# Compacting the first group's token rows with float32 products instead of split parts, with unread TensorE passes around the ranking

## The chip, the cores and the metric

One core of a Trainium2 chip (trn2) runs the whole program. The metric is the device time of one execution in microseconds (us), lower is better. The engines named below are TensorE (PE, with its weight loads PEld), VectorE (DVE), ScalarE (ACT), GpSimd (POOL) and SyncE (SP), which here only issues DMAs.

## What is computed

One step of a one-layer streaming encoder for 384 tokens of width 1024 (256 of a prompt, 128 of a decode batch): a combined projection, three attention-like branches, gates, an output projection with residual, and then a hierarchical mixture of experts. The change lies between the last two:

```python
x = x + merged @ w_out
return x + hier_moe(rmsnorm(x, g_norm2), ...)

def hier_moe(h, ...):
    lg = (t @ w_rg + b_rg).astype(F32)
    oh_g = one_hot(argmax(lg), N_GROUPS)          # top 1 of 4 groups
    le = (t @ w_re + b_re) ; le_sel = le of the chosen group
    top_v, top_i = lax.top_k(le_sel, TOP_K)       # top 2 of its 8 experts
    comb = p(group) * softmax(top_v) on these experts
    out = sum over experts of (silu(t @ w_g) * (t @ w_u) * comb) @ w_d
```

An expert has gate and up weights of 1024 x 256 each and down weights of 256 x 1024, all float32.

## The kernel before, in words

All engines walk through two lists written out in Python, `schedule()` for everything up to the routing and `moe_schedule()` for the experts. Each engine runs the same list and takes from it only its own operations, in that order, so an entry's place sets the order in every queue. Semaphores tie the engines together.

**Products.** The dense projections split each operand into a high part in the reduced type fp32r and a low part (the rest) and make three single-pass products of them (L1579 to L1581). Expert products, logits and transposes use plain float32 (L1919, L1942, L1847).

**The end of `schedule()`.** The output projection runs in two halves of 512 columns; its last weight granule is followed by the second residual (DVE L1287), the transposes of x2 (PE L1839), the norm (DVE L1294 to L1296) and the second half of the logits (PE L1847). `x_parts` splits the residual rows x2 into x_hi and x_lo: half 0 by ACT (L1068) and DVE (L1301); of half 1 the high part by ACT, while PE subtracts it (`second_low`, L1598 with the identity as float32, L1599 with the negated identity as fp32r) and ACT copies the result out (L1072). `route` is `route_group` on DVE (L689 to L707: which of the 4 groups each token takes; L693 writes that one-hot for PE) and, on PE, `token_ranks` (L1590, L1592: how many earlier tokens took the same group). DVE reads these ranks at L704.

**The start of `moe_schedule()`.** The up to 128 tokens of a group are its "opening set" of rows. DVE builds a 0/1 matrix pick_g that maps tokens to the group's slots (L1313). PE multiplies it with the rows of x2, for group 0 out of x_hi and x_lo (`compact`, L1880, three token tiles by two parts for each 512 columns); ACT scales the result by the token's norm into xg_hi (L1082), DVE makes xg_lo (`compact_low`, L1324). Meanwhile DVE finds the two best experts (`best`, L678 to L721), PE ranks the tokens in each expert (L1590 again), DVE turns the ranks into slots (`slots`, L727 to L734), PE brings slots and weights into the group's order (`info`, L1890), DVE builds pick_rows (L1353, L1354), and PE gathers and turns the rows for the first four experts (`gather`, L1905), which ACT (L1103) and DVE (L1361) bring out of PSUM into xs.

**The experts.** 16 pairs: gate and up products in two halves (L1919, `gu` and `gu_rest`), silu and weight, transposes (L1928), down products (L1942), scatter back (L1951). The weights come as 96 pieces of 1 MB through a ring of 17 slots; SP issues them in order (L786). Pieces 0 to 11 go out during the output projection. Piece 15 waits for both compactions (L873), since it lands where x2 lies. From piece 17 on each waits until the piece 17 places before has been used: by the first gate/up half (`gu_half`), the second (`gu_ready`) or the down products (`dn_ready`) of its pair.

```python
old = c - PIECES
sp.wait_ge((gu_half, gu_ready, dn_ready)[old % 6 // 2], old // 6 + 1)
```

Of the kernel before, what the change touches and what calls it, by code (L numbers as in the profile page):

```python
# [26 lines left out]
ALU = mybir.AluOpType  # L27
# [5 lines left out]
P = 128  # L33
# [49 lines left out]
def schedule():  # L83
# [143 lines left out]
    s += [("x_parts", 0), ("logits", 0)]  # L227
    granule(b + 3)
    s += [("residual", 1), ("squares2", 1), ("turn_x2", 1), ("norm2",), ("logits", 1), ("x_parts", 1), ("route",)]
# [3 lines left out]
def moe_schedule():  # L233
# [16 lines left out]
    step("compact", 0, 1, 1)  # L250
    s.append(("compact_low", 0, 0, 0, None))
    plain("slots", 0)
    s.append(("compact_low", 0, 1, 1, None))
# [64 lines left out]
def program(nc, io):  # L318
# [4 lines left out]
    with ctx:  # L323
# [39 lines left out]
        def sm(n):  # L363
# [82 lines left out]
        x_hi = [[at(f"x_hi{n}{t}", [P, 512], (o_raw, o_ot)[n] + 2 * KB * t, F32R) for t in range(T)] for n in range(2)]  # L446
        x_lo = [[at(f"x_lo{n}{t}", [P, 512], ((o_raw + 6 * KB, o_raw + 8 * KB, o_raw + 10 * KB), (o_ot + 6 * KB, o_ot + 8 * KB, o_h + 8 * KB))[n][t], F32R)
                 for t in range(T)] for n in range(2)]
        xs = at("xs", [P, 2, KT, 256], o_raw)
        neg_ident = at("neg_ident", [P, P], o_z + 111 * KB, F32R)  # L450
# [54 lines left out]
        out_tile, xlo_psum = sem("out_tile"), sem("xlo_psum")  # L505
        gate_ready, br_mul, br_add, mt_ready, mt_hi, mt_evac, x2_ready, ss2_ready, rstd2_ready = (sem(n) for n in ("gate_ready", "br_mul", "br_add", "mt_ready", "mt_hi", "mt_evac", "x2_ready", "ss2_ready", "rstd2_ready"))
        x2t_ready, x2t_even, x2t_odd, lg_ready, route_in, route_exp, taken_ready, rank_ready, info_in = (sem(n) for n in ("x2t_ready", "x2t_even", "x2t_odd", "lg_ready", "route_in", "route_exp", "taken_ready", "rank_ready", "info_in"))
        rows_ready, rows_out, xhi_ready, xparts_ready, pick_ready, gather_done, xs_even, xs_odd, gu_ready = (sem(n) for n in ("rows_ready", "rows_out", "xhi_ready", "xparts_ready", "pick_ready", "gather_done", "xs_even", "xs_odd", "gu_ready"))
# [386 lines left out]
        def _(act):  # L895
            for kind, *arg in steps:
# [165 lines left out]
                elif kind == "x_parts":  # L1062
                    if i == 0:
                        act.activation(neg_ident[:, :], ident, ACT.Copy, scale=-1.0)
                        act.wait_ge(lo_ready, NGRAN)
                    act.wait_ge(x2_ready, T * i + T)
                    for t in range(T):
                        act.activation(x_hi[i][t][:, :], x2[:, t, 512 * i:512 * i + 512], ACT.Copy).then_inc(xhi_ready, 1)  # L1068
                    if i == 1:
                        for t in range(T):  # L1070
                            act.wait_ge(xlo_psum, t + 1)
                            act.activation(x_lo[i][t][:, :], ps[:, t, :], ACT.Copy).then_inc(xparts_ready, 1)  # L1072
# [501 lines left out]
        def _(pe):  # L1574
# [26 lines left out]
            for kind, *arg in steps:  # L1601
# [251 lines left out]
                elif kind == "route":  # L1853
                    token_ranks(0, 32, 4, [T * NR + 4 * t for t in range(T)])
                    second_low(2)
# [258 lines left out]
```

## Time and profile before

| | us |
|---|---|
| median of 3 runs | 685.89 |
| lowest and highest run | 685.65, 686.43 |
| the profiled execution, its own time | 685.87 |
| its span in the profile | 684.1 |
| DVE, ACT, POOL busy | 348.6, 255.9, 117.8 |
| bytes moved, mean rate | 176.65 MB, 258 GB/s |

The rows further down come from this one profiled execution. In a timeline a row is the start, the duration, the engine, the line of the code, the operation, what it writes and reads, its shape and how often, and in brackets how long the engine had been idle before and on whom it had waited. Start times count from the start of the span. A float32 product shows as two records on PE, an fp32r product as one. A matmul's record is longer than its share of the engine, because consecutive ones overlap; the spacing of the starts is the price of one in a stream.

### The profile page before, as it was taken

How to read it: one execution, taken by the hardware profiler on the slowest of the kernel's cores; microseconds unless marked ns; L12 is line 12 of the kernel's file. 1: busy time of each engine (PE TensorE's matmuls, PEld its weight loads, DVE VectorE, ACT ScalarE, POOL GpSimd, SP SyncE). 2: the span in 40 equal slices, each digit the busy share in tenths (PEclk: the TensorE clock that was granted, in tenths of full speed). 3: DMA queues.
4: the chain of work that ended last, by engine and by line, in shares of the span. 5: the costliest groups of instructions: out<-in, count | busy, mean ns of one | idle time of the engine just before them, and what ended most of it. 6: DMA issues, size and time to landing. Idle time of an engine off the chain costs nothing.

```text
span 684.1 us, 9466 instructions
## 1 busy us (share of the span) xinstructions
PE 647.9 (95%) x3518; PEld 430.2 (63%) x3518; DVE 348.6 (51%) x743; ACT 255.9 (37%) x495; POOL 117.8 (17%) x128
## 2 busy tenths in 40 slices
PE   5999999998999999999999999978999999999985
PEld 4887888877788776777777878753433443343321
DVE  4649348985446555554445755565434344343212
ACT  5673343336324545455854334321211221221100
POOL 0019426652001110000000010002101201201100
PEclk9999999999999999999999999999999999999999
DMA  8966342354123632213676479978999999999991
GB/s 313 409 239 211 129 131 94 142 202 140 63 85 130 224 125 98 89 62 124 248 276 262 138 248 423 405 306 333 425 420 419 421 422 419 421 423 419 422 418 54
DMA packets 34703, 176.65 MB, mean 258 GB/s; under 512 B 4272, under 2 KB 4416, under 8 KB 21472
## 3 DMA queue, kind: packets, MB, share of 16 engines
q1 hardware_dynamic: 31696, 164.86, 61.8%
q0 software_dynamic: 2960, 11.16, 4.7%
q8 instruction: 30, 0.49, 0.3%
q14 instruction: 17, 0.14, 0.1%
HBM read 167.47 MB, written 9.06 MB: 258 GB/s over the span
## 4 chain that ended last, share of the span: by engine, by line
PE 78%; issue 8%; DVE 6%; DMA 4%; ACT 2%; POOL 0%; POOLq 0%; SPq 0%; DVEq 0%; ACTq 0%
PE banks L1919 14%; PE banks L1579 14%; PE banks L1581 13%; PE banks L1580 13%; PE banks L1942 8%; DMA piece<-in_wexp 4%; PE banks L1905 2%; PE banks L1773 1%; PE banks L1746 1%; PE banks L1787 1%; PE banks L1847 1%; DVE xs L1361 1%; DVE act_T L1389 1%; PE banks L1747 1%; PE banks L1765 1%
## 5 line engine op out<-in xcount | busy, mean ns | idle before, releaser
L1160 DVE TENSOR_TENSOR w_lo<-raw,w_hi 128x1024 fp32r<-128x1024 f32 (+1 forms) x81 | 128.5, 1597 | 87.9 <-ACT w_hi L926 87.7
L1579 PE MATMUL banks<-w_hi,hT_hi 128*128 128x512 f32 x312 | 124.0, 397 | 1.5 <-ACT z L953 0.9
L1581 PE MATMUL banks<-w_hi,hT_lo 128*128 128x512 f32 x312 | 121.6, 390 | 0.0
L1580 PE MATMUL banks<-w_lo,hT_hi 128*128 128x512 f32 x312 | 121.6, 390 | 0.0
L1919 PE MATMUL banks<-piece,xs 128*64 128x512 f32 x512 | 116.1, 594 | 3.0 <-DMA piece<-in_wexp 2.9
L926 ACT ACTIVATE w_hi<-raw 128x1024 fp32r<-128x1024 f32 x79 | 83.4, 1056 | 88.6 <-PE banks L1581 84.5
L1919 PEld LDWEIGHTS banks<-piece,xs 128*64 128x64 f32 x512 | 37.8, 137 | 77.5 <-issue 69.7
L1579 PEld LDWEIGHTS banks<-w_hi,hT_hi 128*128 128x128 f32 x312 | 58.6, 188 | 15.3 <-issue 2.0
L1581 PEld LDWEIGHTS banks<-w_hi,hT_lo 128*128 128x128 f32 x312 | 58.6, 188 | 12.4
L1580 PEld LDWEIGHTS banks<-w_lo,hT_hi 128*128 128x128 f32 x312 | 58.6, 188 | 11.4
L1942 PE MATMUL banks<-piece,act_T 128*64 128x512 f32 x256 | 60.2, 613 | 1.2 <-DVE act_T L1389 0.3
L1394 DVE SCALAR_TENSOR_TENSOR act_h<-banks,rt,act_g 128x256 f32<-128x256 f32 x16 | 7.7, 484 | 76.2 <-ACT act_g L1109 76.1
L1377 DVE TENSOR_TENSOR y_lo<-banks,y_hi 128x512 fp32r<-128x512 f32 x32 | 20.6, 686 | 48.7 <-ACT y_hi L1114 48.7
L1114 ACT ACTIVATE y_hi<-banks 128x512 fp32r<-128x512 f32 x32 | 17.4, 595 | 74.4 <-PE banks L1942 74.4
L1942 PEld LDWEIGHTS banks<-piece,act_T 128*64 128x64 f32 x256 | 17.3, 139 | 34.9 <-issue 29.2
L1109 ACT ACTIVATE act_g<-banks 128x256 f32<-128x256 f32 x16 | 6.2, 385 | 84.8 <-PE banks L1919 84.8
L1551 POOL TENSOR_SCALAR back<-slotrow,const 128x128 fp32r<-128x128 f32 x16 | 10.0, 627 | 121.3 <-ACT slotrow L1088 60.3
L1579 PE MATMUL banks<-w_hi,oT_hi 128*128 128x512 f32 x72 | 28.9, 401 | 1.4 <-DVE oT_lo L1272 1.4
L1581 PE MATMUL banks<-w_hi,oT_lo 128*128 128x512 f32 x72 | 28.1, 390 | 0.0
L1580 PE MATMUL banks<-w_lo,oT_hi 128*128 128x512 f32 x72 | 28.1, 390 | 0.0
L953 ACT ACTIVATE z<-banks,small 128x512 f32<-128x512 f32 x39 | 23.8, 683 | 4.6 <-PE banks L1581 3.0
L997 ACT ACTIVATE p_sb<-s_sb,small 128x256 f32<-128x256 f32 (+1 forms) x24 | 11.4, 475 | 32.0 <-DVE small L1250 32.0
(340 smaller groups left out, 979.8 us busy)
## 6 DMA issues: line engine op xcount, KB each, us to landing
piece<-in_wexp SPq DMA_DIRECT2D x96, 1024.0 KB, 19.5
raw<-in_wstream SPq DMA_DIRECT2D x79, 512.0 KB, 4.2
foxc<-in_foxc POOLq DMA_DIRECT2D x8, 512.0 KB, 4.9
memv<-in_memc SPq DMA_DIRECT2D x8, 512.0 KB, 4.8
memk<-in_memc SPq DMA_DIRECT2D x8, 512.0 KB, 4.9
xT<-in_xT SPq DMA_DIRECT2D x1, 1536.0 KB, 11.5
xtok<-in_xtok SPq DMA_DIRECT2D x1, 1536.0 KB, 7.8
x<-in_xtok SPq DMA_DIRECT2D x1, 1536.0 KB, 6.2
```

Of the source, the lines that this page charges most:

```text
L926: act.activation(w_hi[:, i % PART_SLOTS, :], raw[:, i % RAW_SLOTS, :], ACT.Copy).then_inc(hi_ready, 1)
L953: act.activation(dst[:, t, :], ps[:, bank_of(i, t), :], f, scale=sc).then_inc(acc_evac if last else tile_evac[t], 1)
L997: act.activation(p_sb[:, i % 2, 0:n], src, ACT.Exp, bias=nmax[:, i % 2:i % 2 + 1], accum_out=rsum[:, i % 2:i % 2 + 1]).then_inc(u_exp, 1)
L1114: act.activation(y_hi[:, 512 * n:512 * n + 512], ps[:, 5 + n, :], ACT.Copy).then_inc(yhi_ready, 1)
L1160: dve.tensor_tensor(w_lo[:, i % PART_SLOTS, cols], raw[:, i % RAW_SLOTS, cols], w_hi[:, i % PART_SLOTS, cols].bitcast(F32), ALU.subtract). ...
L1377: dve.tensor_tensor(y_lo[:, cols], ps[:, 5 + n, :], y_hi[:, cols].bitcast(F32), ALU.subtract).then_inc(ylo_ready, 1)
L1579: mm(out, xh, wh, start=start, stop=False, skip_group_check=True)
L1580: mm(out, xh, wl, start=False, stop=False, skip_group_check=True)
L1581: return mm(out, xl, wh, start=False, stop=stop, skip_group_check=True)
L1905: ins = mm(ps[:, b0, 256 * k2:256 * k2 + 256], x[:, k * P:(k + 1) * P], pick[:, :], start=x is xg_hi, stop=x is xg_lo, **kw)
L1919: ins = mm(ps[64 * e2:64 * e2 + 64, 2 + a % 2, :], xs[:, (a // 2) % 2, k, c0:c0 + CAP], piece[c % PIECES][:, 512 * (k % 4):512 * (k % 4) + ...
L1942: ins = mm(ps[64 * e2:64 * e2 + 64, 5 + n, :], act_T[:, a % 2, f * P + 64 * e2:f * P + 64 * e2 + 64], piece[c % PIECES][:, o:o + 512], sta ...
```

## The change

`x_parts` is dropped: no x_hi, x_lo or negated identity is made, on any engine. `compact` multiplies pick_g, read as float32, with x2 itself, three float32 products for each 512 columns in place of six fp32r ones; it no longer waits for parts. The compaction of the second 512 columns is moved behind `slots` in the list of the experts, so behind the ranks of the experts on PE and behind the slots on DVE. PE gets products whose result nobody reads (384 columns, fp32r, into bank 3): six behind the second half of the logits and four behind the ranks of the groups, where `second_low` was. In the overflow branch the count that PE waits for is lowered to match; that branch isn't taken in these runs. The diff:

```diff
--- before.py
+++ after.py
@@ -224,9 +224,9 @@
     granule(b + 1)
     s.append(("turn_x2", 0))
     granule(b + 2)
-    s += [("x_parts", 0), ("logits", 0)]
+    s.append(("logits", 0))
     granule(b + 3)
-    s += [("residual", 1), ("squares2", 1), ("turn_x2", 1), ("norm2",), ("logits", 1), ("x_parts", 1), ("route",)]
+    s += [("residual", 1), ("squares2", 1), ("turn_x2", 1), ("norm2",), ("logits", 1), ("route",)]
     return s, units
 
 
@@ -247,9 +247,9 @@
     plain("info", 0)
     plain("best", 0, 1)
     step("compact", 0, 0, 0)
-    step("compact", 0, 1, 1)
     s.append(("compact_low", 0, 0, 0, None))
     plain("slots", 0)
+    step("compact", 0, 1, 1)
     s.append(("compact_low", 0, 1, 1, None))
     plain("info", 1)
     plain("pick", 0)
@@ -443,11 +443,7 @@
         y_lo = at("y_lo", [P, D], o_z + 100 * KB, F32R)
         xrow = [at(f"xrow{i}", [P, D], o_z + (104 + 4 * i) * KB) for i in range(2)]
         assert o_z + 113 * KB <= end
-        x_hi = [[at(f"x_hi{n}{t}", [P, 512], (o_raw, o_ot)[n] + 2 * KB * t, F32R) for t in range(T)] for n in range(2)]
-        x_lo = [[at(f"x_lo{n}{t}", [P, 512], ((o_raw + 6 * KB, o_raw + 8 * KB, o_raw + 10 * KB), (o_ot + 6 * KB, o_ot + 8 * KB, o_h + 8 * KB))[n][t], F32R)
-                 for t in range(T)] for n in range(2)]
         xs = at("xs", [P, 2, KT, 256], o_raw)
-        neg_ident = at("neg_ident", [P, P], o_z + 111 * KB, F32R)
         sq_scratch = at("sq_scratch", [P, 512], o_z + 108 * KB)
         xg_hi = at("xg_hi", [P, D], o_h, F32R)
         xg_lo = at("xg_lo", [P, D], o_h + 4 * KB, F32R)
@@ -502,10 +498,10 @@
...
@@ -1059,17 +1055,6 @@
                     for j in range(4 * i + 1, 4 * i + 4, 2):
                         act.wait_ge(x2t_ready, j + 1)
                         act.activation(h2T[:, j, :], ps[:, TURN_BANK[j], 0:TOK], ACT.Copy, scale=gk[:, 16 + j:17 + j]).then_inc(x2t_odd, 1)
-                elif kind == "x_parts":
-                    if i == 0:
-                        act.activation(neg_ident[:, :], ident, ACT.Copy, scale=-1.0)
-                        act.wait_ge(lo_ready, NGRAN)
-                    act.wait_ge(x2_ready, T * i + T)
-                    for t in range(T):
-                        act.activation(x_hi[i][t][:, :], x2[:, t, 512 * i:512 * i + 512], ACT.Copy).then_inc(xhi_ready, 1)
-                    if i == 1:
-                        for t in range(T):
-                            act.wait_ge(xlo_psum, t + 1)
-                            act.activation(x_lo[i][t][:, :], ps[:, t, :], ACT.Copy).then_inc(xparts_ready, 1)
 
             for what, a, j, bank, _ in moe:
                 if what == "weights":
@@ -1295,10 +1280,6 @@
                     chain(dve.tensor_scalar(ss2[:, 0:T], ss2[:, 0:T], 1.0 / D, EPS, ALU.mult, ALU.add))
                     rsqrt(dve, chain, rstd2, ss2[:, 0:T], T).then_inc(rstd2_ready, 1)
                     dve.wait_ge(rstd2_ready, 1)
-                elif kind == "x_parts" and i == 0:
-                    for t in range(T):
-                        dve.wait_ge(xhi_ready, t + 1)
-                        dve.tensor_tensor(x_lo[i][t][:, :], x2[:, t, 0:512], x_hi[i][t][:, :].bitcast(F32), ALU.subtract).then_inc(xparts_ready, 1)
                 elif kind == "route":
                     route_group(dve, chain)
 
@@ -1580,6 +1561,11 @@
                 mm(out, xh, wl, start=False, stop=False, skip_group_check=True)
                 return mm(out, xl, wh, start=False, stop=stop, skip_group_check=True)
 
+            def unread_passes(n):
+
+                for _ in range(n):
+                    mm(ps[:, 3, 0:TOK], mT_hi[:, 0, 0:P], mT_hi[:, 1, :], start=True, stop=True, skip_group_check=True)
+
             def token_ranks(part, c0, n, out):
 
                 kw = dict(skip_group_check=True)
@@ -1591,12 +1577,6 @@
                 for u in range(T):
                     ins = mm(ps[0:1, 7, c0:c0 + n], ones_b[:, 0:1], taken_b[:, NR * u + c0:NR * u + c0 + n], start=u == 0, stop=u == 2, **kw)
                 ins.then_inc(rank_ready, 1)
-
-            def second_low(t):
-
-                pe.wait_ge(xhi_ready, T + t + 1)
-                mm(ps[:, t, :], ident, x2[:, t, 512:1024], start=True, stop=False, skip_group_check=True)
-                mm(ps[:, t, :], neg_ident[:, :], x_hi[1][t][:, :], start=False, stop=True, skip_group_check=True).then_inc(xlo_psum, 1)
 
             for kind, *arg in steps:
                 i = arg[0] if arg else 0
@@ -1847,12 +1827,10 @@
                             ins = mm(ps[:, LOGITS, 36 * t:36 * t + 36], h2T[:, k, t * P:(t + 1) * P], wr[:, k, :], start=k == 0 and t == 0, stop=k == KT - 1, skip_group_check=True)
                     if i:
                         ins.then_inc(lg_ready, 1)
-                elif kind == "x_parts" and i == 1:
-                    second_low(0)
-                    second_low(1)
+                        unread_passes(6)
                 elif kind == "route":
                     token_ranks(0, 32, 4, [T * NR + 4 * t for t in range(T)])
-                    second_low(2)
+                    unread_passes(4)
 
             kw = dict(skip_group_check=True)
 
@@ -1874,10 +1852,8 @@
                 bank_free(old)
                 if what == "compact":
                     pe.wait_ge(pick_group, 1)
-                    pe.wait_ge(xparts_ready, 2 * T if j else T + 1)
                     for t in range(T):
-                        for x in (x_hi, x_lo):
-                            ins = mm(ps[:, b0, :], pick_g[:, t, :], x[j][t][:, :], start=t == 0 and x is x_hi, stop=t == 2 and x is x_lo, **kw)
+                        ins = mm(ps[:, b0, :], pick_g[:, t, :].bitcast(F32), x2[:, t, 512 * j:512 * j + 512], start=t == 0, stop=t == 2, **kw)
                     ins.then_inc(compact_done, 1)
                 elif what == "info":
                     pe.wait_ge(info_in, min(a, 2) + 1)
@@ -1952,7 +1928,7 @@
                     ins.then_inc(sc_ready, 1)
             with if_overflow(pe):
                 pe.wait_ge(acc_done, 2 * NG + 2)
-                pe.wait_ge(xhi_ready, 2 * T + 1)
+                pe.wait_ge(xhi_ready, 1)
                 pe.wait_ge(s_x2, 96)
                 for k in range(KT):
                     for t in range(T):
```

## Rows read from the trace of the kernel before

**Rows 1.** The page, busy time, share of the span and instructions of the engines.

```profile
PE 647.9 (95%) x3518; PEld 430.2 (63%) x3518; DVE 348.6 (51%) x743; ACT 255.9 (37%) x495; POOL 117.8 (17%) x128
```

**Rows 2.** Chain of waits near the end: start, us, what.

```profile
627.43 3.65 PE banks L1942 x16
...
639.51 26.09 DMA piece<-in_wexp
```

**Rows 3.** Stretches: length, PE, PEld, DVE, ACT, POOL busy, clock, DMA share, GB/s.

```profile
456.00:460.50 4.50, 3.80 (x22) 1.47 (x17) 1.91 (x15) 0.00 (x0) 0.00 (x0) 1.00 0.28 66
471.00:476.00 5.00, 5.00 (x22) 1.64 (x20) 1.29 (x2) 1.09 (x2) 2.41 (x4) 0.83 0.63 156
480.00:640.00 160.00, 158.49 (x776) 66.29 (x773) 61.15 (x172) 34.53 (x72) 25.78 (x41) 1.00 1.01 421
```

**Rows 4.** Timeline of PE at the first gather.

```profile
451.69 0.38 PE L1905 MATMUL banks<-pick_rows,xg_hi 128*128 128x256 f32 x1 [1.36 <-DVE pick_rows L1354]
...
453.55 0.41 PE L1905 MATMUL banks<-pick_rows,xg_hi 128*128 128x256 f32 x1
453.76 0.41 PE L1905 MATMUL banks<-pick_rows,xg_lo 128*128 128x256 f32 x1
...
455.11 0.91 PE L1919 MATMUL banks<-piece,xs 128*64 128x512 f32 x2
```

**Rows 5.** Timeline of PE from the logits to the compaction.

```profile
438.60 2.06 PE L1598 MATMUL banks<-x,const 128*128 128x512 f32 x2
...
442.54 0.18 PE L1590 MATMUL banks<-taken_b,before_b 128*128 128x4 bf16 x1
...
442.92 1.12 PE L1598 MATMUL banks<-x,const 128*128 128x512 f32 x2
443.48 0.80 PE L1599 MATMUL banks<-x_hi,neg_ident 128*128 128x512 f32 x1
...
444.87 0.48 PE L1880 MATMUL banks<-x_hi,pick_group 128*128 128x512 f32 x1
...
447.50 0.39 PE L1880 MATMUL banks<-x_lo,pick_group 128*128 128x512 f32 x1
```

**Rows 6.** Timeline of DVE in the same stretch.

```profile
440.54 0.17 DVE L693 CAST taken_b<-rt 128x12 bf16<-128x12 f32 x1
...
441.40 0.17 DVE L700 TENSOR_TENSOR info_parts<-small,info_parts 128x3 fp32r<-128x3 f32 x1
443.03 0.17 DVE L704 TENSOR_TENSOR rt<-banks,const 128x12 f32<-128x12 f32 x1 [1.46 <-PE banks L1592]
...
443.72 0.68 DVE L1313 TENSOR_SCALAR pick_group<-const,rt 128x128 fp32r<-128x128 f32 x3
...
447.55 0.74 DVE L1324 SCALAR_TENSOR_TENSOR xg_lo<-banks,rt,xg_hi 128x512 fp32r<-128x512 f32 x1
448.23 0.26 DVE L727 TENSOR_TENSOR rt<-banks,const 128x96 f32<-128x96 f32 x1
...
449.85 0.74 DVE L1324 SCALAR_TENSOR_TENSOR xg_lo<-banks,rt,xg_hi 128x512 fp32r<-128x512 f32 x1
```

**Rows 7.** Stretches as in rows 3, for the granted clock (third number from the end).

```profile
438.60:442.00 3.40, 3.40 (x8) 1.75 (x7) 2.54 (x15) 0.60 (x1) 0.00 (x0) 0.50 1.06 405
448.80:452.20 3.40, 1.01 (x7) 0.92 (x8) 2.60 (x8) 0.00 (x0) 0.00 (x0) 1.00 1.02 429
452.30:455.60 3.30, 3.22 (x16) 2.73 (x16) 1.41 (x4) 1.87 (x6) 0.00 (x0) 0.50 1.02 429
469.40:472.70 3.30, 3.30 (x10) 0.98 (x8) 1.05 (x8) 0.00 (x0) 1.97 (x3) 0.50 0.67 231
```

**Rows 8.** Instructions on the tile x_lo, shortest/median/longest ns, first and last start.

```profile
L1301 DVE TENSOR_TENSOR x_lo<-x,x_hi x3: 684/686/693, 424.5 to 425.7; 128x512 fp32r<-128x512 f32 x3
```

**Rows 9.** Timeline of ACT, the scaling of compaction 0.

```profile
446.54 0.69 ACT L1082 ACTIVATE xg_hi<-banks,rt 128x512 fp32r<-128x512 f32 x1 [1.63 <-PE banks L1880]
```

**Rows 10.** Waits of SP's queue: us in total, times, longest.

```profile
SPq L873 <- PE banks L1880: 7.1, 1, 7.1
```

More of the change, by code:

```diff
@@ L504, in program @@
         second_half_in = sem("second_half_in")
-        out_tile, xlo_psum = sem("out_tile"), sem("xlo_psum")
+        out_tile = sem("out_tile")
         gate_ready, br_mul, br_add, mt_ready, mt_hi, mt_evac, x2_ready, ss2_ready, rstd2_ready = (sem(n) for n in ("gate_ready", "br_mul", "br_add", "mt_ready", "mt_hi", "mt_evac", "x2_ready", "ss2_ready", "rstd2_ready"))
         x2t_ready, x2t_even, x2t_odd, lg_ready, route_in, route_exp, taken_ready, rank_ready, info_in = (sem(n) for n in ("x2t_ready", "x2t_even", "x2t_odd", "lg_ready", "route_in", "route_exp", "taken_ready", "rank_ready", "info_in"))
-        rows_ready, rows_out, xhi_ready, xparts_ready, pick_ready, gather_done, xs_even, xs_odd, gu_ready = (sem(n) for n in ("rows_ready", "rows_out", "xhi_ready", "xparts_ready", "pick_ready", "gather_done", "xs_even", "xs_odd", "gu_ready"))
+        rows_ready, rows_out, xhi_ready, pick_ready, gather_done, xs_even, xs_odd, gu_ready = (sem(n) for n in ("rows_ready", "rows_out", "xhi_ready", "pick_ready", "gather_done", "xs_even", "xs_odd", "gu_ready"))
         pick_group, compact_done, info_done, info_out, xg_hi_ready, xg_lo_ready = (sem(n) for n in ("pick_group", "compact_done", "info_done", "info_out", "xg_hi_ready", "xg_lo_ready"))
```

## The prediction, made before the result was known

> **What bounds it now.** I read the page first: PE is busy 95% of the span [rows 1]. That alone would make every pass worth its time, so I asked what the end waits for. In the chain of waits PE carries the time up to 638 us, and then for 26.09 us nothing but the arrival of expert weights [rows 2]. The cut by stretches says how that comes about [rows 3]: from 480 to 640 the transfers run at share 1.01 and 421 GB/s, so no work of PE there moves the end. But they were starved before: share 0.28 from 456 to 460.5 and 0.63 from 471 to 476, because all 17 slots of the ring were full and pair 0 of the experts had not yet freed one. So the last byte lands a fixed time after pair 0 has done its gate/up and down products, and whatever moves these moves the end one for one. Pair 0's first products start at 455.11 [rows 4]; before it lies the stage that the diff edits.
>
> That stage (438.6 to 455) is a ping-pong of PE, DVE and ACT. PE, in its timeline [rows 5]: the identity products for the low parts from 438.60, right behind the logits, the ranks of the groups (442.54), the third low part (442.92), compaction with its first pass at 444.87 and its last at 447.50. Then DVE [rows 6]: the one-hot of the groups is ready at 440.54 + 0.17 = 440.71, DVE is through with its own list at 441.57, and yet the next line starts only at 443.03, since the ranks stood in PE's queue behind the low parts. That is a stall of 1.46 us. From then on DVE is never idle until the gather: 443.03 (ranks read), 443.72 (pick), the search for the two best experts, 447.55 (low half 0), 448.23 (slots), 449.85 (low half 1).
>
> The granted clock [rows 7]: 0.50, which is 1.2 GHz, from 438.6 to 442.0, after the logits (narrow products); again from 452.3, after a stretch in which PE was busy 1.01 of 3.4 us; and from 469.4. Each low stretch in these rows lasts some 3.4 us.
>
> **Removed, with no gain of its own.** The identity products, x_hi of half 1 and the copies of x_lo leave. x_lo of half 0 (and x_hi just before it) ran from 424.5 to 426.4, beside the output projection's products, so they cost nothing; with that cover gone they would be three subtractions of 0.69 us on DVE [rows 8]. x_hi of half 1 ran on ACT while DVE made the norm.
>
> **The ranks come earlier.** PE now has 6 unread passes of 384 columns after the logits. At 1.2 GHz one costs between 0.21 (256 columns, the gather's spacing from 453.55 to 453.76 [rows 4]) and 0.48 (512 columns, twice the full-clock spacing worked out below); by columns 0.32, so 1.9 us, 438.65 to 440.6. They are done before the one-hot at 440.71, hence free; at 0.48 they would end at 441.5 and DVE would go on some 0.5 us late, which the high end has to cover. The ranks take 0.49 us at full clock (442.54 to DVE's start at 443.03), at most twice that here: ready between 441.25 and 441.7. DVE goes on at 441.60 in place of 443.03: **-1.43 us**. The pick matrix is complete at 442.97, not 444.40. The 4 further passes (0.16 to 0.32 each) are over by 442.4: free as well. The 9 fewer ACT operations were on nobody's path.
>
> **The compaction gets dearer.** Per half, 6 single passes become 3 float32 products. The old passes are 11 spacings in 2.63 us, 0.24 each [rows 5]. For a float32 product of 128x512 on the full clock there are two prices. The third low part: 442.92 to 443.48 + 0.80 = 444.28, less one pass (0.39), is 0.97, or 0.88 without the 0.09 of a first start. The down products of a pair: 8 of them, each on half the array, in 3.65 us [rows 2], so 0.91 for a full one. I take 0.91, a steady stream as here; ends 0.88 and 0.97. A half then costs 2.73 against 1.43. (The page "FP8 and Floating Point Precision" of the Trainium skill, section "TensorE Precision Notes", counts four passes through the array for true FP32; by that and the 0.24 of the old passes a product would be 0.96 and the sum 0.7 us later than before, inside the ends here.)
>
> **The new chain**, offsets as in the rows. Compaction 0 begins 0.47 after the pick (444.40 to 444.87): 443.44, streams until 446.17, drains at 446.33. ACT scales it (0.69 [rows 9]): 447.06. DVE's low half takes 447.10 to 447.78 (447.55 to 448.23 before [rows 6]), and slots start there. DVE's own list would have allowed the low half at 446.12 (447.55 - 1.43), so of the 1.43 us only 0.45 are left: the high half is late now. The experts' ranks are behind compaction 0 on PE and take 0.38 of it (442.54 to 442.92): 446.55. The moved compaction 1 begins only now: until 449.28, drained 449.45. ACT until 450.18, DVE's low half 1 at 450.22, where it stood at 449.85: **+0.37 us**. Slots end 0.45 earlier than before, so DVE idles over 0.7 us there: compaction 1 has become the bound. Queued behind that wait on DVE are the info reduce and the pick of rows, for which the gather on PE waits. The info product of PE is behind compaction 1 too, but DVE reads it only after its low half, so it loses nothing. With 0.88 and 0.97 per product the result is +0.19 and +0.73.
>
> SP's queue: pieces 15 and 16 wait for the second compaction (7.1 us [rows 10]); they go 1.5 us later, near 449.5. Before, the transfers ran dry at about 456; these two pieces are 2.1 MB, 5.0 us at 421 GB/s, so the queue ahead of them lasts to 451: hidden. If it weren't, the idle time from 456 on would take it up. Nothing on POOL moves.
>
> **To the end.** The gather starts at 452.06 (451.69 before). Pair 0 follows 0.94 behind the end of the 12th pass (453.76 + 0.41 = 454.17 to 455.11 [rows 4]): ACT has to bring the bank out. If the clock falls at 452.3 as before, the 12 passes are 11 spacings of 0.21 and 0.41: 454.78, and pair 0 begins at 455.72, 0.61 later. But before it ran at half clock until 455.65 and lost 0.27 by that; now it loses nothing. The net is +0.34 to +0.37. The low stretch at 469.4 falls into the same down products. The profiled execution has a span of 684.1 and a time of 685.87; 685.87 + 0.37 = **686.2 us**, 0.35 above the median 685.89. About 0.2%, 1.37 us, is what a measurement can tell.
>
> **Rivals.**
> Clock kept, faster. Compaction 1 now reaches to 449.45, and the time without wide products shrinks from 3.8 us (447.89 to 451.69) to 2.6. If the clock doesn't fall at 452.3, the gather's 12 passes at half the spacing end at 453.7, and pair 0 starts near 454.7 in place of 455.72: 686.2 - 1.0 = 685.2. Pair 0's down products would then stand more in the stretch up to 469.3 as well; if that fall goes too, it gives half of 3.4 us, 683.5. Against it: the share of wide products before 452.3 hardly changes, 0.5 us of one kind for 0.5 of another.
> The Trainium skill, "TensorE: Matmul & The Clock Gate", section "Why this matters for your kernels", asks that PE be left no long idle gaps between bursts of products, or the clock drops; a shorter gap speaks for this rival. The fall at 452.3 agrees with that; no row shows a gap of the new length.
> Clock not restored, slower. Before, PE was busy without a break from 438.6 to 442.0 with products that streamed 512 columns, and the clock rose. Now there are six passes, a pause and tiny products. If the low stretch lasts twice as long, to 445.4, compaction 0 has 1.06 of its 3 products at 1.82 us each and ends at 447.2, not 446.17: +1.0, so 687.3; with 0.97 per product 687.7. It decides where the clock is still 0.50 at 443.5, when compaction 0 starts. For it: no row shows such passes.
> Ranks not earlier. If the passes hold the ranks as the low parts did, the 1.43 is missing and only the dear products remain: 687.7.
> The stage is hidden anyway: if the transfers made up for it, 685.9. Against: they are at their rate from 480 on.
>
> **Chances.** Forecast 0.44 (its own range 685.9 to 686.7). Clock kept 0.25: 0.08 for 685.2, 0.17 for a time more than 0.2% below. Clock not restored 0.20: 0.11 beyond 0.2%, 0.09 inside. Ranks not earlier 0.07, slower. Hidden 0.04. Faster 0.17; same 0.44 + 0.08 + 0.09 + 0.04 = 0.65; slower 0.18. The range leaves out only the 0.17: low end 685.2 less 0.2 (price 0.88) less 0.2 (the lowest timed run is that far below the median), 684.8; high end 687.7 and 0.2 more for the unread passes and the spread, 687.9.
>
> **What would show it.** In the changed profile: DVE's line after the first ranks at about 441.6 and no stall of 1.5 us before it; two blocks of three float32 products (six records), 2.7 us each, about 443.4 and 446.6; a wait of DVE of about 0.7 us for ACT before the second low half; the gather near 452.1; clock 0.50 from 438.6 to 442.0; SP's wait for compaction near 8.5 us; transfers full from 476. Wrong if the gather starts before 451.5 or after 453, or if the two low stretches behind 450 are gone.

## The result, and the profile after

Ten runs of each kernel on the same chips: 688.32 us median for the changed kernel, 685.15 us for the one before. The ratio is 1.005, with a 95% interval of 1.0036 to 1.0064: slower, by about 3.2 us, and outside the range that was given. The profiled execution of the changed kernel has a time of 688.46 and a span of 686.7, against 685.87 and 684.1 before, so it shows 2.6 us of the difference. In a few jobs one run was far longer than the others (2263 us in e4, 937 in e8, 931 for the kernel before beside e12): it is left out of the ratios, which go by the other runs, but counted in the medians as given.

The page first, which answers to [rows 1]:

```profile
PE 650.1 (95%) x3519; PEld 430.8 (63%) x3519; DVE 346.5 (50%) x740; ACT 250.7 (37%) x485; POOL 116.7 (17%) x128
```

PE is as busy as before, and DVE's 348.6 and ACT's 255.9 us have become 346.5 and 250.7. Both engines have less to do and the kernel is slower, so their work is not what the time hangs on.

PE's timeline from the logits to the gather, which answers to [rows 5] and [rows 4] (start, duration, line, operation; the six unread passes are the first row, the ranks of the groups the second):

```profile
438.71 1.29 PE L1567 MATMUL banks<-mT_hi 128*128 128x384 f32 x6
440.84 0.18 PE L1576 MATMUL banks<-taken_b,before_b 128*128 128x4 bf16 x1 [0.84 <-DVE taken_b L689]
...
441.22 1.65 PE L1567 MATMUL banks<-mT_hi 128*128 128x384 f32 x4
443.07 0.77 PE L1866 MATMUL banks<-info_parts,pick_group 128*128 128x4 f32 x3 [0.20 <-DVE pick_group L1294]
443.70 4.98 PE L1856 MATMUL banks<-x,pick_group 128*128 128x512 f32 x6
448.51 0.18 PE L1576 MATMUL banks<-taken_b,before_b 128*128 128x32 bf16 x1
...
448.91 2.84 PE L1856 MATMUL banks<-x,pick_group 128*128 128x512 f32 x6
...
454.36 0.38 PE L1881 MATMUL banks<-pick_rows,xg_hi 128*128 128x256 f32 x1 [2.17 <-DVE pick_rows L1335]
```

And DVE's, which answers to [rows 6]:

```profile
440.62 0.17 DVE L689 CAST taken_b<-rt 128x12 bf16<-128x12 f32 x1
...
441.56 0.16 DVE L700 TENSOR_TENSOR rt<-banks,const 128x12 f32<-128x12 f32 x1
...
442.24 0.68 DVE L1294 TENSOR_SCALAR pick_group<-const,rt 128x128 fp32r<-128x128 f32 x3
...
449.44 0.75 DVE L1305 SCALAR_TENSOR_TENSOR xg_lo<-banks,rt,xg_hi 128x512 fp32r<-128x512 f32 x1 [3.26 <-ACT xg_hi L1067]
450.11 0.25 DVE L723 TENSOR_TENSOR rt<-banks,const 128x96 f32<-128x96 f32 x1
...
452.51 0.75 DVE L1305 SCALAR_TENSOR_TENSOR xg_lo<-banks,rt,xg_hi 128x512 fp32r<-128x512 f32 x1 [0.71 <-ACT xg_hi L1067]
```

Read the two together. The ranks are read at 441.56, where they had been read at 443.03, as the forecast had it (441.60). The pick matrix is ready at 442.92. Up to here the change is 1.5 us ahead. Then compaction 0 stands on PE from 443.70, and the next instruction starts only at 448.51: 4.81 us for three float32 products, 1.60 each, where I had taken 0.91. The second one takes (451.69 is the start of the info product behind it) 2.78, 0.93 each. So DVE's first low half comes at 449.44, not 447.10, and the gather at 454.36, not 452.06.

The stretches of the granted clock, cut as in [rows 7] (third number from the end):

```profile
437.80:441.20 3.40, 2.56 (x25) 2.21 (x24) 2.86 (x17) 0.00 (x0) 0.00 (x0) 1.00 1.06 406
441.30:444.60 3.30, 3.10 (x8) 2.20 (x9) 2.88 (x20) 0.00 (x0) 0.00 (x0) 0.50 1.07 400
444.70:448.00 3.30, 3.30 (x5) 1.34 (x4) 1.34 (x8) 0.00 (x0) 0.00 (x0) 0.50 1.01 416
...
454.70:458.10 3.40, 3.32 (x18) 3.03 (x18) 1.20 (x3) 1.88 (x6) 0.00 (x0) 0.53 1.01 419
480.00:640.00 160.00, 158.49 (x775) 65.53 (x773) 60.36 (x170) 33.41 (x69) 25.70 (x41) 1.00 1.01 421
```

0.50 is 1.2 GHz, 1.00 is 2.4 GHz. Before, one low stretch covered the identity products and ended at 442.0. Here PE stays at full clock through the logits and the six passes, falls at 441.2, and is low for 6.8 us, until 448.1. All of compaction 0 but its end lies in it. The low stretch of the gather is there as before.

The stream behind it is unchanged: 421 GB/s from 480 to 640 (last row), and the chain of waits ends on the same 26 us of weights, 2.6 us later than in [rows 2]:

```profile
642.12 26.08 DMA piece<-in_wexp
```

The first down products of pair 0 start at 471.19 and take 5.35 (low clock again):

```profile
471.19 5.35 PE L1918 MATMUL banks<-piece,act_T 128*64 128x512 f32 x16
```

They end at 476.54, and the span is 686.7: 210.2 us from one to the other. Before, the same row stood at 468.52 with the same 5.35, end 473.87, and the span was 684.1: also 210.2 us. So the 2.6 us of the stage went through to the end whole. SP's wait for the second compaction [rows 10] was

```profile
SPq L869 <- PE banks L1856: 10.8, 1, 10.8
```

3.7 us longer, and the transfers show it (share 0.98 against 1.02 of their time from 434 to 452), but they waited for pair 0 afterwards anyway: the distance from pair 0's down products to the end hasn't changed.

### The profile page after: what moved, and what is told of

It is laid out like the page before. It is cut to its first block, busy times and chain, and to the rows that moved or that the text cites. A ratio compares the mean times of both kernels' runs of the same rounds, so it can differ in the third digit from the quotient of the medians.

```text
span 686.7 us, 9452 instructions
## 1 busy us (share of the span) xinstructions
PE 650.1 (95%) x3519; PEld 430.8 (63%) x3519; DVE 346.5 (50%) x740; ACT 250.7 (37%) x485; POOL 116.7 (17%) x128
## 4 chain that ended last, share of the span: by engine, by line
PE 79%; issue 8%; DVE 6%; DMA 4%; ACT 2%; POOL 0%; POOLq 0%; SPq 0%; DVEq 0%; ACTq 0%
PE banks L1895 14%; PE banks L1560 14%; PE banks L1562 13%; PE banks L1561 13%; PE banks L1918 8%; DMA piece<-in_wexp 4%; PE banks L1881 2%; PE banks L1753 1%; PE banks L1856 1%; PE banks L1726 1%; PE banks L1767 1%; PE banks L1827 1%; DVE xs L1342 1%; DVE act_T L1370 1%; PE banks L1727 1%
```

## The experiments

The kernels were timed in turns with the kernel before, whose median in these jobs lay between 685.46 and 685.83. Two theories to begin with: A, that the loss is the half clock during compaction 0, because PE has too little wide work ahead of it; B, that the products and their order cost this much at any clock. A third, C, was that the unread passes are in the way.

**e1: more unread passes.**

```diff
-                        unread_passes(6)
+                        unread_passes(12)
...
-                    unread_passes(4)
+                    unread_passes(10)
```

> The changed kernel with 12 unread passes behind the logits in place of 6, and 10 behind the first ranks in place of 4, so that PE has hardly a pause from the logits to the compaction. Theory A (the half clock during compaction 0 is the loss, because PE has too little wide work before it): the clock is back at 2.4 GHz when compaction 0 runs, its three float32 products take 2.7 us and not 4.8, the gather starts at 452.0 to 452.8 against 454.4 in the changed kernel, and the time falls by 1 to 2.5 us to about 686 to 687.3. Theory B (the dearer products and their order are the loss at any clock): no change, 688.3 within 0.5. Theory C (the unread passes are in the way): slower than the changed kernel, by up to 2 us, since the passes may hold back the first ranks at half clock.

686.53 us, ratio to the kernel before 1.0021 (1.0006 to 1.0036): 1.8 us faster than the changed kernel. PE's timeline:

```profile
438.44 2.33 PE L1567 MATMUL banks<-mT_hi 128*128 128x384 f32 x12
...
440.99 2.01 PE L1567 MATMUL banks<-mT_hi 128*128 128x384 f32 x10
...
443.13 2.82 PE L1856 MATMUL banks<-x,pick_group 128*128 128x512 f32 x6
445.80 0.19 PE L1576 MATMUL banks<-taken_b,before_b 128*128 128x32 bf16 x1
...
446.20 2.84 PE L1856 MATMUL banks<-x,pick_group 128*128 128x512 f32 x6
...
451.65 0.38 PE L1881 MATMUL banks<-pick_rows,xg_hi 128*128 128x256 f32 x1 [2.19 <-DVE pick_rows L1335]
```

Both compactions now take the same: 443.13 to 445.80 and 446.20 to 448.96 (the info product), 0.89 and 0.92 a product. The gather starts at 451.65. A holds, and C falls: 12 more passes that nobody reads make the kernel faster. B falls as it was put (no change), but only as the whole of the loss: 0.9 us against the kernel before are left in the medians, and e9 and e12 below show what the products cost at full clock. This profile is also one of the faster runs, 685.06: of the eleven times three lie at 688.7 to 688.9, so the passes don't keep the clock up in every run.

**e2: none.**

```diff
-                        unread_passes(6)
...
-                    unread_passes(4)
```

> The changed kernel with no unread passes at all. Theory A: with even less work before the compaction it is at half clock throughout as now, possibly for longer: the same as the changed kernel or up to 1 us slower (688.3 to 689.3). Theory B: the same, 688.3. Theory C: faster, 687.5 or less.

688.92 us, ratio 1.0056 (1.0041 to 1.0071). The clock by stretches, and compaction 0:

```profile
438.90:449.00 10.10, 6.82 (x27) 3.36 (x28) 6.03 (x37) 0.22 (x1) 0.00 (x0) 0.50 1.04 396
449.10:455.40 6.30, 4.07 (x16) 2.31 (x17) 3.87 (x11) 1.20 (x3) 0.00 (x0) 1.00 0.71 257
```

```profile
443.28 5.47 PE L1854 MATMUL banks<-x,pick_group 128*128 128x512 f32 x6
```

One low stretch of 10.1 us. Whether the ten passes of the change do anything isn't shown: the medians differ by 0.6 us (688.92 and 688.32), but the intervals of the two ratios overlap (1.0041 to 1.0071 and 1.0036 to 1.0064), and this profile, 687.71, is faster than that of the changed kernel, 688.46.

**e3: the moved compaction put back.**

```diff
+    step("compact", 0, 1, 1)
     s.append(("compact_low", 0, 0, 0, None))
     plain("slots", 0)
-    step("compact", 0, 1, 1)
```

> The changed kernel with the compaction of the second 512 columns back in front of the slots. At half clock PE then has six float32 products in a row before the ranks of the experts. Theory A: compaction 1 delays the ranks and the slots; the gather starts about 0.5 us earlier or later, and the loss of 2 to 3 us against the kernel before stays. Theory B with its share in the order: if putting compaction 1 behind the slots is what costs, this gives back 1 us or more (687.3 or less).

689.72 us, ratio 1.0064 (1.0049 to 1.0079), 1.4 above the changed kernel:

```profile
443.50 8.28 PE L1856 MATMUL banks<-x,pick_group 128*128 128x512 f32 x12
451.62 0.18 PE L1576 MATMUL banks<-taken_b,before_b 128*128 128x32 bf16 x1
...
455.58 0.38 PE L1881 MATMUL banks<-pick_rows,xg_hi 128*128 128x256 f32 x1 [1.37 <-DVE pick_rows L1335]
```

Twelve records, six products, are 8.1 us from 443.50 to the ranks of the experts at 451.62, so the slots wait, and the gather comes 1.2 us later than in the changed kernel. The expectation, about 0.5 us earlier or later, missed that. The move is the good part of the change, as long as the products are this dear; its size is open, since the intervals of the two ratios overlap and the low stretch in this profile lasts from about 439 to 449.3, longer than the changed kernel's 6.8 us.

**e4: the float32 products alone, in the kernel before.**

```diff
-                        for x in (x_hi, x_lo):
-                            ins = mm(ps[:, b0, :], pick_g[:, t, :], x[j][t][:, :], start=t == 0 and x is x_hi, stop=t == 2 and x is x_lo, **kw)
+                        ins = mm(ps[:, b0, :], pick_g[:, t, :].bitcast(F32), x2[:, t, 512 * j:512 * j + 512], start=t == 0, stop=t == 2, **kw)
```

> The kernel before with only the products of the compaction changed to float32 from x2; parts and identity products stay, and so does the order. PE is then fed from the logits to the compaction. Theory A: both compactions run at full clock in nearly every run, 2.7 us each in place of 1.4, the gather starts 1 to 2 us later than before, and the time is 1 to 1.8 us above the kernel before, about 686.5. Theory B: the same size as the whole change, 2.5 to 3.5 us above before.

686.84 us, ratio 1.0025 (1.0012 to 1.0038), 1.2 us above the kernel before:

```profile
438.45 1.52 PE L1598 MATMUL banks<-x,const 128*128 128x512 f32 x2
...
442.33 0.23 PE L1590 MATMUL banks<-taken_b,before_b 128*128 128x4 bf16 x1
...
444.70 5.40 PE L1879 MATMUL banks<-x,pick_group 128*128 128x512 f32 x12
449.94 0.18 PE L1590 MATMUL banks<-taken_b,before_b 128*128 128x32 bf16 x1
```

With the identity products in place the clock is up when the compaction starts, although it was low in them: 5.24 us for six products, 0.87 each. That speaks for the removed identity products as what had fed PE, though it is one profile, 1.3 us above the median (688.15), with a low stretch of 6.8 us at the gather (452.5 to 459.3) that reaches into the first products of pair 0.

**e5: more passes behind the ranks only**, 6 behind the logits as in the change.

```diff
-                    unread_passes(4)
+                    unread_passes(10)
```

> The changed kernel with 6 unread passes behind the logits as it has, and 10 behind the first ranks in place of 4: one half of e1_fill. Theory A (PE has too little wide work before compaction 0, so that it runs at half clock) and the passes behind the ranks are the ones nearest to it: between the changed kernel and e1_fill, 687 to 687.8. If the passes only have to be in the right place, all of e1_fill's gain, 686.5. Rival (the passes behind the ranks delay info and the pick, at half clock by up to 1.4 us): no gain or slower, 688.3 to 689.

686.61 us, ratio 1.002 (1.0009 to 1.0031): all of e1's gain. The profile shows what it costs to buy the clock this way:

```profile
440.96 3.57 PE L1567 MATMUL banks<-mT_hi 128*128 128x384 f32 x10
...
444.82 3.35 PE L1856 MATMUL banks<-x,pick_group 128*128 128x512 f32 x6
448.01 0.18 PE L1576 MATMUL banks<-taken_b,before_b 128*128 128x32 bf16 x1
...
456.48 3.65 PE L1895 MATMUL banks<-piece,xs 128*64 128x512 f32 x16 [0.45 <-ACT xs L1088]
```

The ten passes ran at 1.2 GHz, 3.6 us, and held compaction 0 back to 444.82. It then takes 3.19 us instead of 4.81 and ends 0.5 us earlier than in the changed kernel. That is the smaller part of what this profile (686.96) gains on the changed kernel's: its gather, from 453.86, runs at full clock (granted 1.00 from 453.5 to 457), so pair 0 starts at 456.48 and not at 457.82, 1.3 us earlier. The next low stretch comes only at 469.5.

**e6: early ranks without float32.** The kernel before, with these moves.

```diff
                 elif kind == "x_parts" and i == 1:
-                    second_low(0)
-                    second_low(1)
+                    unread_passes(12)
                 elif kind == "route":
                     token_ranks(0, 32, 4, [T * NR + 4 * t for t in range(T)])
+                    second_low(0)
+                    second_low(1)
                     second_low(2)
```

> The kernel before (parts, single-pass products) with all three identity products moved behind the ranks of the groups and 12 unread passes in front of the ranks: the early ranks without the float32 compaction. Ranks read at 441.6, the identity products end near 444.7 at full clock, compaction 0 near its old place, slots at 447.7 in place of 448.2. Theory A: 0.3 to 0.8 us faster than the kernel before, about 685; where the clock is low in the identity products, up to 1.5 us slower. Rival (what the early ranks give is always 1.4 us): 684.2.

687.24 us, ratio 1.0021 (1.0007 to 1.0035): slower than before. Both theories missed; the loss is as large as what theory A allowed for a low clock in the identity products, but here they ran at full clock.

```profile
438.45 3.76 PE L1586 MATMUL banks<-mT_hi 128*128 128x384 f32 x12
442.01 0.23 PE L1595 MATMUL banks<-taken_b,before_b 128*128 128x4 bf16 x1
...
442.44 1.13 PE L1603 MATMUL banks<-x,const 128*128 128x512 f32 x2
```

The passes took 3.6 us at the low clock and held the ranks up to 442.01, about where they had been, and now all three identity products stand in front of the compaction. In this profile the early ranks never came about, so it doesn't tell what they are worth.

**e7: PE fed at the later waits too.** e1 with these calls (8 between info and gather, 8 and 3 around the transposes of pair 0):

```diff
+            def late_passes(n, bank, w, x):
+                for _ in range(n):
+                    mm(ps[:, bank, 0:384], w, x, start=True, stop=True, skip_group_check=True)
...
+                    if a == 1:
+                        late_passes(8, 3, pick_g[:, 0, :], pick_g[:, :, :])
...
+                    if a == 0:
+                        late_passes(8, 5, xg_hi[:, 0:P], xg_hi[:, 0:384])
                     pe.wait_ge(h_ready, a + 1)
...
+                    if a == 0:
+                        late_passes(3, 5, xg_hi[:, 0:P], xg_hi[:, 0:384])
```

> e1_fill with further unread passes where PE waits later: 8 between the info product and the gather, 8 and 3 around the transposes of pair 0 before its first down products. If low stretches there cost half their length where PE is what the chain waits for (1.0 us at the gather, 1.7 us at the down products of pair 0, by the rows of before), the time falls by 1.5 to 3 us against e1_fill (686.5), to 683.5 to 685. If those stretches are hidden by the transfers or the passes delay what follows: no change, 686.5, or slower.

685.28 us, ratio 0.9995 (0.9982 to 1.0008), 1.25 us faster than e1 (the expectation began at 1.5). The profile, 683.67, has no low stretch at all from 434 to the last weights, and the first down products take 3.65 us, not 5.35:

```profile
467.34 3.65 PE L1931 MATMUL banks<-piece,act_T 128*64 128x512 f32 x16
```

It is the fastest of the twelve runs. Four more lie below 684.1, five at 685.3 to 685.4 and two near 687, so at the median, 685.28, something is left that this profile doesn't have.

**e8: the late passes of e7 in the kernel before**, and 8 more behind the ranks of the experts, where compaction 1 stands in the changed kernel.

```diff
                     token_ranks(1, 0, 32, [NR * t for t in range(T)])
+                    if True:
+                        late_passes(8, 3, pick_g[:, 0, :], pick_g[:, :, :])
```

> The kernel before with unread passes only at the later places: 8 behind the ranks of the experts, 8 between info and gather, 8 and 3 around the transposes of pair 0. Nothing in the changed stage up to the ranks is touched. The same theory: 1.5 to 2.7 us faster than the kernel before (685.6), to 683 to 684. Otherwise no change.

683.83 us, ratio 0.997 (0.9956 to 0.9985): 1.9 us faster than the kernel before. This beats both kernels, without anything of the change. The median falls between two groups of times, six at 682.1 to 682.7 and five at 684.9 to 685.4. The profile, 685.07, is from the second, and it has two low stretches, not one: besides 440.6 to 444.1, in the identity products, one long before the edited stage.

```profile
229.00:233.00 4.00, 4.00 (x25) 2.94 (x23) 1.72 (x6) 2.20 (x6) 0.00 (x0) 0.57 0.55 221
```

So the transposes of x2 start at 435.32 here, where they start at 433.85 in the kernel before and in e9. I overlooked that when I wrote the expectation of e9.

**e9: e8 with 5 passes in front of the second half of the logits.**

```diff
                 elif kind == "logits":
                     pe.wait_ge(s_route_in, 32)
+                    if i:
+                        for _ in range(5):
+                            mm(ps[:, 0, 0:TOK], mT_hi[:, 0, 0:P], mT_hi[:, 1, :], start=True, stop=True, skip_group_check=True)
```

> e8_before_latefill (the kernel before with the later unread passes) with 5 more unread passes in front of the second half of the logits, where PE waits half a microsecond for the transposed rows. The times of e8 lie in two groups, near 682.2 and near 685.1; its profile, 685.07, has one low stretch left, 440.6 to 444.1, in the identity products. If the second group is the runs with that stretch, filling the pause makes it rarer: median near 682.5 to 683.5, though the passes may cost up to 0.5 us on the path. If the two groups have another cause, the share of the second stays, with a median as e8's, 683.8, or higher.

682.28 us (681.89 to 682.79), ratio 0.9957 (0.9945 to 0.997): 3.2 us faster than the kernel before, the best of the study. None of its five times lies in the second group of e8. But the five passes come long after the low stretch at 229 and can't have removed it, and if they did nothing, five runs out of five in the first group (six of eleven in e8) would still come about once in 20 times, by my estimate. So how much of the 1.5 us between e8 and e9 they give is open. The clock is 1.00 in both stretches around the stage:

```profile
435.00:452.00 17.00, 16.62 (x108) 13.22 (x107) 13.75 (x66) 7.31 (x15) 0.00 (x0) 1.00 1.02 397
452.00:476.00 24.00, 22.61 (x115) 9.89 (x114) 13.07 (x54) 5.23 (x11) 4.85 (x7) 1.00 0.90 345
```

This profile is the kernel before at full clock, and it holds the surprise. PE and DVE:

```profile
438.76 1.10 PE L1603 MATMUL banks<-x,const 128*128 128x512 f32 x2
...
441.03 0.18 PE L1595 MATMUL banks<-taken_b,before_b 128*128 128x4 bf16 x1
...
443.45 0.48 PE L1888 MATMUL banks<-x_hi,pick_group 128*128 128x512 f32 x1
...
450.28 0.38 PE L1917 MATMUL banks<-pick_rows,xg_hi 128*128 128x256 f32 x1
```

```profile
440.68 0.17 DVE L693 CAST taken_b<-rt 128x12 bf16<-128x12 f32 x1
...
441.62 0.16 DVE L704 TENSOR_TENSOR rt<-banks,const 128x12 f32<-128x12 f32 x1
```

The two identity products and their fp32r passes take 2.27 us (438.76 to 441.03), where they had taken 3.94 [rows 5]. So the ranks start at 441.03, 0.2 us after the one-hot, and DVE reads them at 441.62 straight after its own list. **There is no stall that the change could remove.** The 1.46 us that I credited to it were the low clock, seen from DVE. (The five passes themselves cost 0.24 us: the logits start at 436.17, against 435.93 before.)

**e10: e3 with more passes behind the ranks**, to have the order at a better clock.

```diff
-                    unread_passes(4)
+                    unread_passes(10)
```

> e3_order_back (compaction 1 in front of the slots again) with 10 unread passes behind the first ranks in place of 4. Against e5_p6_10 (686.6), which has the moved compaction and the same passes, it isolates the move. Theory from the chain: six float32 products in a row end 5.5 us after the pick matrix, so the ranks of the experts and the slots start about 1.1 to 1.5 us later than with the move: 687.5 to 688. If the move costs or gives nothing at full clock: 686.6.

687.52 us, ratio 1.0035 (1.002 to 1.0051), 0.9 above e5, which has the same passes and the moved compaction: as in e3, the move is worth something. How much stays open here too: the intervals overlap (e5's is 1.0009 to 1.0031), the profiles have the gather 0.47 us apart (454.33 and 453.86), and this one has a low stretch at the gather, from 455 to 459, that e5's lacks.

**e11 and e12: the change with PE fed everywhere.** e11 is e5 with the late passes and those in front of the logits; e12 differs from it by

```diff
-                        unread_passes(6)
+                        unread_passes(12)
```

> e5_p6_10 with the later unread passes of e7 and the 5 passes in front of the logits of e9: the change with PE fed everywhere. Against e9 it shows what the change is worth when the clock is out of the question. By the forecast's sum (products 0.9 us each, early ranks 1.4 us): 0 to 0.7 us slower than e9, about 683.5. If the change itself (dear products, order) costs more than that at full clock: 685 or more.

> e11 with 12 unread passes behind the logits in place of 6, which closes the last pause of PE, 439.9 to 440.8 in e11's profile. The times of e11 lie near 684.2 and near 685.6; its profile, from the first group, has the gather 1.60 us later than e9's and no low stretch. Theory: at full clock the change costs these 1.6 us, all of them in the compaction chain, and e11's second group is runs with one low stretch left. Then the median here is 684.0 to 684.4, 1.7 to 2.1 above e9, with few runs near 685.6. If the second group stays as it is, the rest of the 3.2 us between the medians of e11 and e9 has a cause that no profile shows.

685.45 us, ratio 1.0002 (0.9991 to 1.0013), and 684.51 us, ratio 0.9987 (0.9976 to 0.9997). Of the twelve times of e12, nine lie between 684.0 and 684.6 and three near 685.8; of e11's eleven, four lay in such a first group. That fits the expectation that the remaining pause made e11's second group, but three runs still are in it, and no profile shows one. Its profile, 684.34, against e9's, 682.79:

```profile
443.51 2.82 PE L1864 MATMUL banks<-x,pick_group 128*128 128x512 f32 x6
...
446.57 2.84 PE L1864 MATMUL banks<-x,pick_group 128*128 128x512 f32 x6
...
452.03 0.39 PE L1893 MATMUL banks<-pick_rows,xg_hi 128*128 128x256 f32 x1 [0.65 <-DVE pick_rows L1335]
```

From the start of compaction 0 to the gather it is 8.52 us here and 6.83 in e9 (443.45 to 450.28). That is 1.69 us, and the profiled times differ by 1.55. At full clock the change costs about 2 us in the medians (684.51 against 682.28), and in the profiles this chain holds all of the difference.

## Why the prediction was wrong, step by step

- **What bounds it: right.** The stage ahead of pair 0 sets the end, the transfers are full behind it. From the end of pair 0's first down products to the end of the span it is 210.2 us in both kernels, 211.1 in e1 (472.24 to 683.3), 210.8 in e7 (470.99 to 681.8) and 211.2 in e9 (469.71 to 680.9). So the tie is one for one between the two kernels; where the down products' own low stretch goes away, 0.6 to 1.0 us of the gain stays behind, which my rows didn't show. It makes the 1.7 us that I gave to that stretch too much.
- **Ranks 1.43 us earlier: right in the profile** (1.47), wrong as a gain of the change. e9 shows the ranks on time with all the identity products in place. I took this term from a stretch at 1.2 GHz. ACT lost ten operations with it (495 to 485), not nine as I wrote, without weight for the sum.
- **Passes free: right.** They were over before the one-hot and before the pick, the first six even at full clock (1.29 us in all, where I had 1.9); where they were many and the clock low (e5, e6), they did hold things up.
- **0.91 us for a product: right at full clock** (0.89 in e1, 0.93 for the second compaction here), and the chain from it: 8.62 us from compaction 0 to the gather as forecast, 8.52 in e12. Whether +0.37 us at the end would have come out with the clock as it was before isn't shown: no run of the changed kernel has that pattern.
- **The step that failed** is the first sentence under "To the end", the gather at 452.06, and the one that it rests on: that the low stretch would lie where it lay before, 438.6 to 442.0, and be over when compaction 0 starts at 443.44. The gather came at 454.36, beyond the 453 that I had named as a sign of being wrong. The sum took a gain from the low clock and its cost from the full one. In the changed kernel the fall came at 441.2 and lasted 6.8 us; compaction 0 took 4.81 us instead of 2.73. That is 2.1 us of the 2.3 by which the gather is later than forecast; the rest is mostly the slow info product ahead of it (0.63 us from 443.07 to 443.70 against 0.33). Of the 3.2 us about 2 are what the change costs at full clock on both sides (e12 against e9); that the rest is the worse place of the low stretch is what the profiles suggest, and no run measures it by itself.
- **The rival "clock not restored"** had the right mechanism and place, with a chance of 0.20, and was mis-sized: it let the stretch begin at 438.6 and last twice as long, so that only 1.9 us of compaction 0 lay in it, +1.0. It lay in it nearly whole, +2.1. I had no row for a low stretch that begins later, though from the start of the logits to compaction 0 there are nearly 8 us (436.04 to 443.70) in which PE does little wide work, and the rows of before show a fall after each such pause.
- **The rival "clock kept"** didn't come about in the changed kernel. As an effect it is real: e7 and e8 bring it about on purpose and gain 1.25 and 1.9 us.
- **The rival "ranks not earlier"** didn't come about either, but its price is the one that fits the change at full clock: 1.8 us for the dear products alone (687.7 against 685.9), and about 2 between e9 and e12. "Hidden" is out: the 2.6 us went to the end whole.
- **SP's queue: hidden, as I said,** though the wait was 10.8 us, not 8.5, since the second compaction came later than forecast.
- **The rule of the Trainium skill** that was weighed, "TensorE: Matmul & The Clock Gate", section "Why this matters for your kernels", no long idle gaps between bursts: e1, e2 and e5 agree with it in their direction (687 and less with more work in the gaps, 688.9 with none). The fall of the changed kernel at 441.2 it doesn't cover: PE's longest pause between the logits and there was 0.84 us (in front of the ranks, 440.84). Whether the change's own passes were enough the rule didn't tell, and they weren't.
- **The median against the profile.** The medians differ by 3.2 us, the profiles by 2.6. Most of that lies with the kernel before: its ten times fall into two groups, five at 684.1 to 684.7 and five at 685.7 to 686.4, its median, 685.15, falls between them, and its profile, 685.87, is from the upper one. The changed kernel's profile, 688.46, is close to its median. Its single times run from 687.5 to 691.1 and go with their mean granted clock: 0.990 for 687.5 to 688.2, 0.984 to 0.986 for 689.4, 0.983 for 691.1. That low stretches fall differently from run to run explains such a spread, as the one at 229 in e8 does there, but of these two kernels no profile shows a second pattern, so this is argued, not shown.

## What to carry to other kernels

Before crediting the removal of work from TensorE, look at the granted clock of the stretch that the numbers come from, and of the one that follows: here the stall that the removed products seemed to cause was made of the low clock, and without them compaction 0 ran at the low clock. Price a change at one clock on both sides, and if the stage has pauses, price it at both. And where the chain waits on TensorE after a pause, products that nobody reads can pay: 32 of them in the kernel before, nearly all in gaps where it waited anyway, gave 3.2 us of 685.5. Too many in one place hold up what follows (e5, e6). And where the times of a kernel fall into groups, find out which group a profile is from before you explain a difference by it.

## What the runs showed of the chip that was not expected

- A low stretch isn't always 3.4 us: it was 6.8 us in the changed kernel and 10.1 in e2. Nor is it always in the same place: e8's profile has one at 229 to 233 that no other profile here has, in products that all the kernels share.
- Kernels that differ only in passes nobody reads differ by 3.2 us in the median (e9 against the kernel before) and by 4.4 (e12 against e2).
- A low stretch can cost less than half its length: the down products of pair 0 lose 1.7 us to one of 3.4 (5.35 against 3.65), and of that the end sees 0.7 to 1.1, by the distances to the end above.
